# Neighbourhood attention in pairs of heads, scores on halves of the array's rows, values on halves of its columns

## The reference

```python
p = h @ w_in
q = axial_rope(p[..., :NA_WIDTH] ...); k = axial_rope(...); v = p[...]
...
s_loc = jnp.einsum("bwhd,brwkhd->bhwrk", q_r, k_win) * scale + bias
s_ctx = jnp.einsum("bwhd,bchd->bhwc", q_r, k_ctx) * scale
scores = jnp.concatenate([s_loc.reshape(bsz, nh, GRID_W, n_loc), s_ctx], axis=-1)
p = jax.nn.softmax(scores.astype(jnp.float32), axis=-1).astype(v.dtype)
return (jnp.einsum("bhwrk,brwkhd->bwhd", p_loc, v_win)
        + jnp.einsum("bhwc,bchd->bwhd", p[..., n_loc:], v_ctx))
...
xs, bm, cm, dt = ssd_prep(p[..., col_ssd:], ssd_conv_w, ssd_conv_b, dt_bias)
y_ssd, _, _ = ssd_bidirectional(p[..., 3 * NA_WIDTH:col_ssd], xs, bm, cm, dt, a, ssd_d, ssd_norm_w, h_fwd, h_bwd)
x = x + g1 * (jnp.concatenate([attn, y_ssd], axis=-1) @ w_out)
```

## Time and profile before

| | |
|---|---|
| median of 3 runs | 2712.24 us (2712.06 to 2713.97) |
| profiled execution | 2716.56 us |
| its span, from the first to the last instruction | 2714.8 us |
| TensorE busy | 2537.0 us, 93% |
| VectorE / ScalarE / GpSimd busy | 1327.0 / 974.9 / 984.1 us |
| mean granted clock of TensorE | 0.969 |

### The profile page before, as it was taken

How to read it: one execution, slowest core, us unless ns; L and a number is a source line. 1 busy time by engine, 2 the same in 40 slices (tenths; PEclk the granted TensorE clock), 3 DMA queues, 4 the chain that set the end, 5 groups by cost and what they waited for, 6 DMA issues and landing times.

```text
span 2714.8 us, 44602 instructions
## 1 busy us (share of the span) xinstructions
PE 2537.0 (93%) x19262; PEld 2253.6 (83%) x19262; DVE 1327.0 (49%) x2039; ACT 974.9 (36%) x1556; POOL 984.1 (36%) x583
## 2 busy tenths in 40 slices
PE   7988988899999999999999999989998998999997
PEld 5877767678888788887999999988987987979896
DVE  4634556363536354444265263466664435635453
ACT  5234334232323444333443332354332234333332
POOL 1734334634444421212535454500001224454544
PEclk9989989999999999999999999999998997999998
DMA  8432120423333221111223223312111012233321
GB/s 248 123 95 60 57 70 1 116 86 93 93 93 89 76 55 39 48 42 45 78 58 99 86 86 94 90 48 70 40 40 32 21 28 63 76 95 86 101 80 60
DMA packets 379923, 201.26 MB, mean 74 GB/s; under 512 B 6464, under 2 KB 377152, under 8 KB 379728
## 3 DMA queue, kind: packets, MB, share of 16 engines
q1 hardware_dynamic: 379728, 198.42, 25.8%
HBM read 196.30 MB, written 2.10 MB: 73 GB/s over the span
## 4 chain that ended last, share of the span: by engine, by line
PE 68%; DVE 16%; ACT 8%; issue 3%; POOL 3%; DMA 1%; POOLq 0%; SPq 0%; ACTq 0%; DVEq 0%
PE ps L661 51%; DVE t_ffy L2859 3%; ACT t_wh L629 2%; DVE t_atq L2653 2%; PE ps L2461 1%; DVE t_wl L639 1%; PE ps L3094 1%; PE ps L2434 1%; DVE t_ffy L2862 1%; PE ps L2400 1%; PE ps L3113 1%; ACT t_ffy L2762 1%; PE ps L1106 1%; PE ps L3117 1%; PE ps L503 1%
## 5 line engine op out<-in xcount | busy, mean ns | idle before, releaser
L639 POOL TENSOR_TENSOR t_wl<-t_raw,t_wh 128x1024 fp32r<-128x1024 f32 (+2 forms) x198 | 448.3, 2265 | 822.0 <-ACT t_wh L629 822.0
L661 PE MATMUL ps<-t_hh,t_wh 128*128 128x264 f32 (+2 forms) x1712 | 404.2, 315 | 12.1 <-DVE t_dcq L2587 3.6
L629 ACT ACTIVATE t_wh<-t_raw 128x1024 fp32r<-128x1024 f32 (+2 forms) x253 | 255.7, 1012 | 424.3 <-PE ps L661 380.1
L661 PE MATMUL ps<-t_hh,t_wl 128*128 128x264 f32 (+2 forms) x1712 | 380.7, 301 | 6.1 <-POOL t_wl L639 3.1
L661 PE MATMUL ps<-t_hl,t_wh 128*128 128x264 f32 (+2 forms) x1712 | 377.1, 301 | 0.0
L661 PEld LDWEIGHTS ps<-t_hh,t_wh 128*128 128x128 f32 x1712 | 271.0, 192 | 34.6 <-issue 17.2
L661 PEld LDWEIGHTS ps<-t_hh,t_wl 128*128 128x128 f32 x1712 | 271.1, 191 | 21.5 <-issue 5.0
L661 PEld LDWEIGHTS ps<-t_hl,t_wh 128*128 128x128 f32 x1712 | 269.7, 191 | 9.1 <-issue 1.5
L639 POOL TENSOR_TENSOR t_fwl<-t_raw,t_fwh 128x1024 fp32r<-128x1024 f32 (+1 forms) x72 | 168.1, 2335 | 165.7 <-ACT t_fwh L629 165.7
L2859 DVE SCALAR_TENSOR_TENSOR t_ffy<-t_ffp,t_vec,t_ffy 128x528 f32<-128x528 f32 (+1 forms) x88 | 177.4, 2016 | 101.5 <-ACT t_ffy L2762 101.5
L661 PE MATMUL ps<-t_fhh,t_wh 128*128 128x512 f32 (+1 forms) x704 | 211.2, 340 | 4.3 <-DVE t_fhl L1769 4.3
(11 more groups left out here) (570 smaller groups left out, 5473.6 us busy)
## 6 DMA issues: line engine op xcount, KB each, us to landing
t_raw<-in_up SPq DMA_DIRECT2D x44, 512.0 KB, 3.9
t_raw<-in_up2a SPq DMA_DIRECT2D x44, 512.0 KB, 3.9
t_raw<-in_up2b SPq DMA_DIRECT2D x44, 512.0 KB, 3.9
t_raw<-in_attn_in SPq DMA_DIRECT2D x33, 512.0 KB, 4.1
t_raw<-in_dn_in SPq DMA_DIRECT2D x33, 512.0 KB, 4.0
t_raw<-in_ada_w SPq DMA_DIRECT2D x32, 512.0 KB, 4.7
t_raw<-in_w_in SPq DMA_DIRECT2D x25, 512.0 KB, 3.9
t_raw<-in_down SPq DMA_DIRECT2D x16, 512.0 KB, 4.0
```

What stands on the lines that cost most here:

```text
L629: ac.activation(wh[slot_of[j]][:, 0:kc, :], raw[r % NRAW][:, 0:kc, :], ACT.Copy).then_inc(up("wh_cut", "cut", j), 1)
L639: eng.tensor_tensor(wl[slot_of[j]][:, 0:kc, :], raw[r % NRAW][:, 0:kc, :], wh[slot_of[j]][:, 0:kc, :].bitcast(F), SUB).then_inc(up(name, " ...
L661: ins = pe.matmul(ps[bank_of(j, i)][:, 0:tn], wt[slot][:, k, :], a[:, k, t0:t0 + tn], start=first, stop=last)
```

## The change

Steps now work on a pair of heads (unit u, 16 in all), and each place holds one step (`ALONE`), at every sixth product in place of every fourth.
- `na_scores(u)` issues the four matmuls of the pair in turns on partitions 0 to 63 and 64 to 127, into two banks, and signals once; VectorE and ScalarE do each head as before. NSC stays 3.
- `na_turn(u)` turns both heads, in two banks, signalled one by one. Both reciprocals are one instruction.
- `na_values(u)` takes the values as stationary operand (64 columns) and the transposed scores as moving operand, head 0 into partitions 0 to 63 and head 1 into 64 to 127, in turns; two more matmuls spread the reciprocals in the same layout. ScalarE copies these out, VectorE multiplies. The output has features on partitions.
- `mix` loses its transposes and banks: four instructions on ScalarE and four on VectorE that read `otm` with a stride.
- GpSimd adds two biases per unit, double buffered by unit; the table is loaded for two heads at a time.

The diff, cut to its core (the removed lines of these functions stand above):

```diff
@@ -963,10 +963,10 @@
+        otm = vflat[:, 0:2048].rearrange("p (m n) -> p m n", m=4)
+        rel = rstd[:, 0:768].rearrange("p (e n) -> p e n", e=2)
...
@@ -978,7 +978,8 @@
+            "na_scores": "biased scored maxed/0 maxed/1 exped/0 exped/1", "na_turn": "turned/0 turned/1 copied/0 copied/1 scaled",
+            "na_values": "weighed copied scaled",
...
@@ -994,18 +995,18 @@
+            for u in range(16 + 2):
+                if u < 16:
+                    put("na_scores", u, banks=2)
+                    if u % 4 == 3 and u < 15:
+                        put("na_rel", u // 4 + 1)
+                    yield ALONE
+                if u >= 2:
+                    put("na_values", u - 2, banks=1)
+                    yield ALONE
+                if 1 <= u < 17:
+                    put("na_turn", u - 1, banks=2)
+                    yield ALONE
...
@@ -1020,8 +1021,8 @@
         put("na_rel", 0)
         put("zero_pads")
         behind.append(na_order())
-        gemm(("xbc",), then_first, every=4)
-        gemm(("z",), then_first, every=4)
+        gemm(("xbc",), then_first, every=6)
+        gemm(("z",), then_first, every=6)
         flush()
         drain()
         sqb_last[:] = [("conved", "conv", 6), ("conved", "conv", 7)]
...
@@ -1041,10 +1042,10 @@
+            def na_rel(m):
+                if m:
+                    w.wait_ge(s.biased, at("biased", "na_scores", 4 * m - 1))
+                sp.dma_start(rel, io["rpb"][2 * m:2 * m + 2].rearrange("e p n -> p e n")).then_inc(s.rel_in, 16)
...
@@ -1075,38 +1076,47 @@
+            def na_scores(u):
+                m, j = divmod(u, 4)
+                bs = bank("na_scores", u)
+                w.wait_ge(s.roped, at("roped", "rope", 7, "3"))
+                for c0, k0 in ((0, 8 * KS[j]), (256, S)):
+                    for e, b in enumerate(bs):
+                        if c0 == 0:
+                            held(b)
+                        p = slice(64 * e, 64 * e + 64)
+                        ins = pe.matmul(ps[b][:, c0:c0 + 256], qT[p, m, 128 * j:128 * j + 128], kT[p, m, k0:k0 + 256],
+                                        start=True, stop=True)
+                ins.then_inc(up("scored", "na_scores", u), 1)
+                for e, b in enumerate(bs):
+                    free[b] = [(s.maxed, at("maxed", "na_scores", u, str(e)))]
+
+            def na_turn(u):
+                for e, b in enumerate(bank("na_turn", u)):
+                    held(b)
+                    w.wait_ge(s.exped, at("exped", "na_scores", u, str(e)))
+                    for k in range(4):
+                        ins = pe.transpose(ps[b][:, 128 * k:128 * k + 128], sco[(2 * u + e) % NSC][:, 128 * k:128 * k + 128],
+                                           C("ident"))
+                    ins.then_inc(up("turned", "na_turn", u, str(e)), 1)
+                    free[b] = [(s.copied, at("copied", "na_turn", u, str(e)))]
+
+            def na_values(u):
+                m, j = divmod(u, 4)
+                b, = bank("na_values", u)
+                w.wait_ge(s.scaled, at("scaled", "na_turn", u))
+                for e in range(2):
+                    pe.matmul(ps[b][64 * e:64 * e + 64, 128:256], rs[:, 2 * u + e:2 * u + e + 1].to_broadcast([128, 64]),
+                              C("ident"), start=True, stop=True)
+                w.wait_ge(s.copied, at("copied", "na_turn", u, "1"))
+                    for e in range(2):
+                        h = 2 * m + e
+                        ins = pe.matmul(ps[b][64 * e:64 * e + 64, 0:128], V[:, v, 64 * h:64 * h + 64],
+                                        pts[e][:, 128 * k:128 * k + 128], start=k == 0, stop=k == 3)
+                ins.then_inc(up("weighed", "na_values", u), 1)
+                free[b] = [(s.scaled, at("scaled", "na_values", u))]
...
@@ -1205,25 +1215,33 @@
+            def na_scores(u):
+                for e in range(2):
+                    i = 2 * u + e
+                    x = sco[i % NSC]
+                    w.wait_ge(s.maxed, at("maxed", "na_scores", u, str(e)))
+                    ac.activation(x[:, :], x[:, :], ACT.Exp, bias=mx[:, i:i + 1],
+                                  accum_out=rs[:, i:i + 1]).then_inc(up("exped", "na_scores", u, str(e)), 1)
+
+            def na_turn(u):
+                for e, b in enumerate(bank("na_turn", u)):
+                    w.wait_ge(s.turned, at("turned", "na_turn", u, str(e)))
+                    if u:
+                        w.wait_ge(s.weighed, at("weighed", "na_values", u - 1))
+                    ac.activation(pts[e], ps[b][:, :], ACT.Copy).then_inc(up("copied", "na_turn", u, str(e)), 1)
+
+            def na_values(u):
+                m, j = divmod(u, 4)
+                b, = bank("na_values", u)
+                w.wait_ge(s.weighed, at("weighed", "na_values", u))
+                ac.activation(otm[:, m, 128 * j:128 * j + 128], ps[b][:, 128:256],
+                              ACT.Copy).then_inc(up("copied", "na_values", u), 1)
+                    "na_values": na_values,
...
@@ -1272,46 +1290,45 @@
+            def na_scores(u):
+                w.wait_ge(s.scored, at("scored", "na_scores", u))
+                w.wait_ge(s.biased, at("biased", "na_scores", u))
+                for e, b in enumerate(bank("na_scores", u)):
+                    i = 2 * u + e
+                    x = sco[i % NSC]
+                    if i >= NSC:
+                        w.wait_ge(s.turned, at("turned", "na_turn", (i - NSC) // 2, str((i - NSC) % 2)))
+                    dv.scalar_tensor_tensor(out=x[:, 0:256], in0=ps[b][:, 0:256], scalar=0.125,
+                                            in1=bias[:, 2 * (u % 2) + e, :], op0=MUL, op1=ADD)
+                    dv.tensor_scalar(x[:, 256:512], ps[b][:, 256:512], 0.125, None, MUL).then_inc(st.up(), 1)
+                    w.wait_ge(st.sem, st.n)
+                    dv.tensor_reduce(mx[:, i:i + 1], x[:, :], AX.X, ALU.max,
+                                     negate=True).then_inc(up("maxed", "na_scores", u, str(e)), 1)
+
+            def na_turn(u):
+                w.wait_ge(s.exped, at("exped", "na_scores", u, "1"))
+                dv.reciprocal(rs[:, 2 * u:2 * u + 2], rs[:, 2 * u:2 * u + 2]).then_inc(up("scaled", "na_turn", u), 1)
+
+            def na_values(u):
+                m, j = divmod(u, 4)
+                b, = bank("na_values", u)
+                o = otm[:, m, 128 * j:128 * j + 128]
+                w.wait_ge(s.copied, at("copied", "na_values", u))
+                dv.tensor_tensor(o, o, ps[b][:, 0:128], MUL).then_inc(up("scaled", "na_values", u), 1)
+            def na_scores(u):
+                m, j = divmod(u, 4)
+                w.wait_ge(s.rel_in, 16 * (m + 1))
+                for e in range(2):
+                    if u >= 2:
+                        w.wait_ge(s.maxed, at("maxed", "na_scores", u - 2, str(e)))
+                    ins = po.tensor_tensor(bias[:, 2 * (u % 2) + e, :], rel[:, e, x0:x0 + 256], mask[:, j, :], ADD)
+                ins.then_inc(up("biased", "na_scores", u), 1)
...
@@ -1546,17 +1560,14 @@
+            return {"rates1": rates1, "turn_s": turn_s, "state": state_, "prep": prep, "yout": yout}
+            def mix(m):
+                w.wait_ge(s.scaled, at("scaled", "na_values", 4 * m + 3))
+                w.wait_ge(s.mm_done, at("mm_done", end_of("z") - 1))
+                ac.activation(by_rows(mh[:, m, 0:S]), by_columns(otm[:, m, :]),
+                              ACT.Copy).then_inc(up("hi_set", "mix", m), 1)
...
@@ -1625,15 +1636,10 @@
+            def mix(m):
+                w.wait_ge(s.hi_set, at("hi_set", "mix", m))
+                dv.tensor_tensor(by_rows(ml[:, m, 0:S]), by_columns(otm[:, m, :]), by_rows(mh[:, m, 0:S]).bitcast(F),
+                                 SUB).then_inc(up("lo_dve", "mix", m), 1)
```

## The result

| | median us | from | to | span of the profiled execution | its own time | mean granted clock |
|---|---|---|---|---|---|---|
| before | 2714.18 (6 runs) | 2712.06 | 2718.75 | 2714.8 | 2716.56 | 0.969 |
| after | 2722.57 (6 runs) | 2720.83 | 2728.81 | 2719.5 | 2722.01 | 0.967 |

The kernel after is slower by 0.35%: ratio 1.0035, 95% interval 1.0025 to 1.0045. The forecast was 2716.3 us with 2700 to 2731 around it, and "within 0.2%" and "slower" were held equally likely. The time came out in the range, 6.3 us above the forecast and on the slower side of the bound.

The account below looks back on a forecast made before the run. TensorE was taken as the bound, but not alone. Work -23.2, waits +25.8, clock +3.0, end -1.5 gave +4.1 us: 2720.7 for the profiled execution, 2716.3 for the median (4.3 lower); range 2700 to 2731.

Parts of the forecast that it names:

- TensorE's work: Attention and products of the stage on TensorE: 169.5 us before, 146.3 us after, saving 23.2 us.
- Waits: TensorE waiting in the stage, since a unit fills two of three score buffers: 40.9 us after, 25.8 more than before.
- panel end, u = 2: First of four panel ends between scores(u) and values(u-2): chain 8.2 us against 3.0 of TensorE's own work, costing 5.2 us.
- seven second transposes: Units with a modulation matmul between scores and transposes: second head's transposes need its new scores' bank; 1.8 us each, 12.5 together.
- values(10) behind Silu: Silu after xbc panel 7 holds the copies values(10) wait for: chain 11.8, cover 6.4, wait 5.4 us.
- the eight smaller ones: Eight waits of 0.4 to 1.6 us at the bank of a copy or a multiply: 6.5 us.
- rival of shorter waits: Engines overlap neighbours or the ring falls otherwise; half the extra waits gone, one clock fall: 2700 us; chance 0.22.
- halves don't overlap: Rival: paired scores and values on TensorE gain no overlap from array halves, 30 us more, 2745 us; chance 0.06.
- Clock: TensorE's falls to 1.2 GHz after idles of 5.2, 6.5, 5.4, 3.4 us: two falls taken, +3.0, bounds -3.0 and +9.0.
- the clock falls at all four: Rival: clock falls at all four long TensorE waits and where shorter ones add up: +6.0 us more, 2722; chance 0.30.
- End of the stage: From last z product to the scan: Silu ends sooner, -1.0, and mix's strided instructions, -0.5; together -1.5 us.
- the dear case: Mix's strided reads of 512 elements cost 1.22 like the rotation's write, not 0.65 each: mix ends 2 us later.

## Why the prediction was right or wrong

**TensorE's work: right, 2.9 us short.** The stage with four buffers is the cleanest measure. From its first product at 175.98 us to the modulation matmul behind the last z product at 336.24 it is 160.3 us. Of these 6.2 are the two waits, 0.5 the tails of them, and 4.4 the lower clock (8.1 us of busy time in two such stretches, half of it lost, and 0.3 in the first product). That leaves 149.2 against my 146.3. Scores of a pair take 1.07 (I had 1.1), values 1.24 (1.37, since going in and out of the halved mode cost 0.17 in place of 0.3), transposes as before; where the 2.9 us come from I cannot say. For the kernel before, the same sum gives 189.1 - 11.2 - 1.2 of tails - 3.9 = 172.8 against 169.5, short by as much. So the work saved is 23.6 us, of the forecast 23.2. The tails are read from start to start: at 202.28 the six instructions come 5.07 us after the first two, which is 4.8 beyond their usual 0.27, and the row says 4.38, hence 0.4 ahead of scores; in the same way 0.2 ahead of the second transposes (2.17 beyond the first at 213.43, usual 0.40, row 1.57) and 0.1 ahead of values (4.91 at 324.87, usual 0.32, row 4.52).

**Waits: right, in place and size.**

| wait of TensorE | forecast us | rows of after, without tails |
|---|---|---|
| panel end, u = 2 | 5.2 | 4.38 |
| u = 6 | 6.5 | 5.68 |
| u = 10 | 3.4 | 2.56 |
| u = 14 | 1.4 | 0.59 |
| seven second transposes | 1.8 each | 1.57 each |
| values(10) behind Silu | 5.4 | 4.52 |
| the eight smaller ones | 6.5 | 3.8, in five rows |
| all | 40.9 | 32.4, with the 17 tails some 37 |

By the ledger (the stage from its first product, less the work of the kernel with four buffers and the lower clock) it is 195.2 - 149.2 - 6.9 = 39.1 us; the 2 us between the two I can't place. Following the written order with the durations of the earlier trace rows gave each of the long waits to within 0.9 us; with the tail added it is 0.4 too long at each panel end and 0.8 at the Silu, and only the small ones came out fewer. For the old order I had 15.1 us, and its rows with their tails are 12.4. The rival of shorter waits (0.22) is out by the traces. That halves don't overlap (0.06) is out by the 1.07 and 1.24.

**Clock: one fall short.** I took two falls and +3.0 us. There are three stretches of 6.8 us with 13.7 us of busy time, half of it lost, 6.9, against 3.0 before: +3.9. That the stage as a whole shows just +3.0 is luck: the first products of the kernel before ran at the lower clock too (0.79 us from start to start in place of 0.44), some 0.9 us, and those of the kernel after did not. The fall that I had not counted belongs to an idle of over 4 us too (I had named four idles and taken two); the one of 2.56 us, forecast at 3.4, brought none. The rival "the clock falls at all four" is therefore out: it wanted 6.0 us more, there were 0.9, and the fourth idle left the clock alone. Its figure, 2722, lies by chance where the median came out.

**End of the stage: wrong by 1.9 us.** From the last z product to the rates it takes 383.30 - 371.60 = 11.7 us, before 376.77 - 365.45 = 11.3: +0.4 where I had -1.5. The step that failed is the 0.65 us for 512 elements read with a stride; it is 1.05, and without the stride 0.54. The Silu is not at fault: it ends 376.62 - 371.60 = 5.0 us after the same mark, where I had 4.8 and the kernel before has 5.9. From there to the rates it is 6.7 us instead of 5.4, +1.3 where I had -0.5. I had carried the dear case as a bound, by the rotation's 1.22, and taken the cheap one with no row for it. The Trainium skill, "SBUF — State Buffer", in its remark on cachelines in the section "Door 1: The DMA port swizzle", says that each access that crosses to a new line of 16 bytes pays a penalty; a stride of 32 bytes does so at each element, and the trace agrees with it by 1.05 against 0.54 us. It gives no factor, but taken ahead it would have spoken for the dear case.

**Sum.** From first product to last the stage is 195.2 us against 189.1: work -23.6, waits +26.7, clock +3.0, together +6.1 (forecast +5.6). With the end +0.4 (-1.5) that is +6.5 us at 383 us, of which 1.8 go again later in the span, in stretches that the change doesn't touch. The profiled execution is 5.45 us longer than that of before, against my 4.1. The other part of the miss is in the step from that execution to the median. I took 4.3 us off because before's profiled execution lay that far above the median of the first three runs. After's lies 0.6 us below its own median. By profiled executions the forecast is 1.3 us off, by medians 6.3, and the difference is these 4.3 and 0.6 us. So most of the miss says nothing of the kernel. The closeness of the 1.3 is in part luck: the 1.9 us too little at the end of the stage stand against the 1.8 that went again, for which I had no term. One execution's distance from a median of three is no property of the kernel, and the scatter of before, 6.7 us over six runs, is as large as the whole effect.

## What to carry to other kernels

When a change makes the steps of a pipeline twice as large, its buffers must be counted in steps: three buffers for two halves is one and a half, and the wait for the missing half sits in the queue of an engine that has other work behind it. Ask for each written wait how many places later its releaser is issued; moving the releaser one place earlier gave back 29 us, and borrowing a buffer that is free until the end of the stage gave back 37. A loss of 0.35% can hide a gain of over 1%, so a change that takes a third of a step's work off the bound engine and saves no time deserves a look at the waits before it is dropped.

## What the runs showed of the hardware that I had not expected

- Two float32 matmuls with 256 moving columns on each half of the rows take 1.07 us together, whether issued in turns or one half after the other; on halves of the columns the order counts, 1.24 against 1.73 us for the values of a pair. The Trainium skill, "TensorE: Matmul & The Clock Gate", Part 3, "What overlaps and what doesn't", says that matmuls start and end strictly in the order of the program. By that I should have expected the scores to take longer with two matmuls of one half ahead of the other half's; the 1.07 us doesn't show it. How the halves come to overlap in that order, no run here shows.
- A read with a stride of 32 bytes makes a ScalarE copy of 512 float32 elements 1.05 us instead of 0.54, while VectorE's multiply of 128 elements with a strided operand in PSUM and runs of 16 in SBUF stays at 287 ns.
- The same length of idle did not always bring the same stretch at the lower clock. With idles of TensorE of 4.38, 5.68 and 4.52 us in the kernel after and of 3.86 us with four buffers came 6.8 us of it, with those of 4.21 and 3.13 us in the kernel before with its heads spread out 3.4 us only. The idle of 2.56 us in the kernel after brought none, one of 2.34 us with four buffers 3.4 us. The windows of the kernel with four buffers show both of its stretches (length, busy PE PEld DVE ACT POOL, granted clock, DMA share, GB/s):

```profile
241.60:245.00 3.40, 3.40 (x11) 2.92 (x12) 2.79 (x6) 2.04 (x4) 3.18 (x3) 0.52 0.00 0
295.70:302.50 6.80, 4.74 (x26) 3.75 (x27) 1.89 (x6) 5.46 (x9) 5.31 (x5) 0.53 0.02 7
```
